# A two-block transformer step on one NeuronCore: joints by token tile, packed narrow weight blocks, and moved gate blocks, rotations and side work

## The reference, cut

```python
# layer 0: gated linear attention, 4 heads
proj = h @ w_in                         # q, k, v, gate and 16 low-rank columns
gk = gk_low @ w_gk2 + b_gk
log_a = jax.nn.log_sigmoid(gk) / 16.0   # cumulated in chunks of 64
o = rms_norm(o, g_onorm)
y = (o * jax.nn.silu(gate)) @ w_out
x = x + rms_norm(y, g_post)             # first joint
# layer 1: latent attention, 16 heads
c_q, c_kv, k_rope, gate = split(h @ w_in, [512, 1024, 1088])
q, kv = rms_norm(c_q) @ w_qb, rms_norm(c_kv) @ w_kvb   # rotations on q_rope, k_rope
p = softmax(mask(q @ k.T * scale)); o = p @ v
y = (o * jax.nn.silu(gate)) @ w_out
x = x + rms_norm(y, g_post)             # second joint
# layer 2: block-sparse attention and a gated delta rule (chunked,
# triangular inverse), merged by gates; then a gated feed-forward net
proj = rms_norm(x) @ w_in               # with 24 and 16 narrow gate columns
x = x + mixed @ w_o
x = x + (silu(h2 @ w_gate) * (h2 @ w_up)) @ w_down
return rms_norm(x, norm_f)
```

## Time and profile before

| | us |
|---|---|
| median of 3 runs (2389.57 to 2391.72) | 2390.56 |
| the profiled execution | 2388.96 |
| its span, first to last instruction | 2387.2 |
| TensorE busy in the span | 2332.0 |
| VectorE, ScalarE busy | 1467.7, 1298.3 |

### The profile page before, as it was taken

How to read it: one execution, slowest core, us unless ns; L and a number is a source line. 1 busy time by engine, 2 the same in 40 slices (tenths; PEclk the granted TensorE clock), 3 DMA queues, 4 the chain that set the end, 5 groups by cost and what they waited for, 6 DMA issues and landing times.

```text
span 2387.2 us, 33365 instructions
## 1 busy us (share of the span) xinstructions
PE 2332.0 (98%) x12514; PEld 1980.5 (83%) x12514; DVE 1467.7 (61%) x2567; ACT 1298.3 (54%) x2397; POOL 18.3 (1%) x38
## 2 busy tenths in 40 slices
PE   8999999899999899999999999999999999999998
PEld 7877788788888899778787888888888888888887
DVE  4554465665565655886777676656666666665554
ACT  5645455565565544775556555546555555554444
POOL 1000000000000000000000000000000000000000
PEclk9999999999999999999999999999999999999999
DMA  6555565556435465656554236656666666665564
GB/s 215 153 167 153 162 204 194 150 151 176 129 118 193 143 185 164 186 169 183 150 168 133 80 98 203 208 180 178 190 188 186 187 189 188 187 205 191 190 190 166
DMA packets 247403, 408.94 MB, mean 171 GB/s; under 512 B 29712, under 2 KB 62528, under 8 KB 246864
## 3 DMA queue, kind: packets, MB, share of 16 engines
q1 hardware_dynamic: 243392, 393.20, 54.4%
q0 software_dynamic: 3136, 10.26, 1.2%
q10 hardware_dynamic: 720, 3.42, 0.4%
HBM read 400.53 MB, written 6.29 MB: 170 GB/s over the span
## 4 chain that ended last, share of the span: by engine, by line
PE 90%; DVE 4%; ACT 4%; issue 1%; DMA 1%; SPq 0%; DVEq 0%; ACTq 0%; POOL 0%; POOLq 0%
PE banks L361 50%; PE banks L335 14%; PE banks L355 9%; PE banks L337 7%; DVE weights_low L306 1%; PE banks L804 1%; ACT weights_high L303 1%; PE banks L644 1%; PE banks L2221 1%; PE banks L2210 1%; PE banks L1681 1%; PE banks L815 0%; DMA weight_ring<-in_w_gla_in 0%; PE banks L1102 0%; PE banks L1112 0%
## 5 line engine op out<-in xcount | busy, mean ns | idle before, releaser
L306 DVE TENSOR_TENSOR weights_low<-weight_ring,weights_high 128x512 fp32r<-128x512 f32 (+3 forms) x1512 | 1006.6, 675 | 831.5 <-ACT weights_high L303 801.4
L303 ACT CAST weights_high<-weight_ring 128x512 fp32r<-128x512 f32 (+3 forms) x1512 | 910.3, 609 | 991.7 <-PE banks L361 624.9
L361 PE MATMUL banks<-weights_high,hidden_T 128*128 128x512 f32 x3008 | 863.9, 399 | 5.8 <-DVE weights_low L306 4.5
L361 PEld LDWEIGHTS banks<-weights_high,hidden_T 128*128 128x128 f32 x3008 | 556.2, 188 | 129.6 <-issue 10.8
L361 PE MATMUL banks<-weights_low,hidden_T 128*128 128x512 f32 x1504 | 466.2, 391 | 0.0
L335 PE MATMUL banks<-hidden_T,weights_high 128*128 128x512 f32 x1408 | 385.1, 394 | 0.6 <-DVE residual L2836 0.6
L361 PEld LDWEIGHTS banks<-weights_low,hidden_T 128*128 128x128 f32 x1504 | 283.0, 188 | 61.4
L335 PEld LDWEIGHTS banks<-hidden_T,weights_high 128*128 128x128 f32 x1408 | 240.4, 189 | 32.9 <-DVE residual L2836 0.8
L337 PEld LDWEIGHTS banks<-hidden_T,weights_low 128*128 128x128 f32 x1408 | 216.5, 189 | 30.3
L337 PE MATMUL banks<-hidden_T,weights_low 128*128 128x256 f32 x1408 | 224.4, 281 | 0.0
L355 PE MATMUL banks<-hidden_T,weights_high 128*128 128x256 f32 (+3 forms) x1120 | 185.8, 287 | 7.3 <-DVE weights_low L306 6.3
(11 more groups left out here) (401 smaller groups left out, 1731.1 us busy)
## 6 DMA issues: line engine op xcount, KB each, us to landing
weight_ring<-in_w_in SPq DMA_DIRECT2D x168, 512.0 KB, 3.6
weight_ring<-in_w_gla_in SPq DMA_DIRECT2D x96, 512.0 KB, 3.8
weight_ring<-in_w_gate SPq DMA_DIRECT2D x88, 512.0 KB, 3.6
weight_ring<-in_w_ffn_up SPq DMA_DIRECT2D x88, 512.0 KB, 3.6
weight_ring<-in_w_down SPq DMA_DIRECT2D x88, 512.0 KB, 3.8
weight_ring<-in_w_mla_in SPq DMA_DIRECT2D x49, 512.0 KB, 3.6
weight_ring<-in_w_gla_out SPq DMA_DIRECT2D x32, 512.0 KB, 3.9
weight_ring<-in_w_mla_out SPq DMA_DIRECT2D x32, 512.0 KB, 4.3
```

The lines of the kernel that those rows point to most:

```text
L303: nc.scalar.copy(hi, raw).then_inc(high_ready, 1)
L306: nc.vector.tensor_tensor(lo, raw, hi.bitcast(F32), ALU.subtract).then_inc(low_ready, 1)
L361: last = pe.matmul(ps[:, b + t, 0:width], a[:, t * P:(t + 1) * P], w, start=(k == 0 and n_th == 0), stop=(k == kt - 1 and n_th == 2))
```

## The change

- Narrow blocks are packed: on the host the columns are laid out so that four input tiles stand side by side (`PACK`), and a narrow chunk has 4 splits of four times the width in place of 16. TensorE issues the same 48 matmuls. The slots after them have lower numbers, so all positions are rewritten. The first block is loaded by ScalarE's queue, ahead of SyncE's.
- Start: the constants ahead are the identity alone, behind the gains, and a small activation stands first. All of x is turned in the first chunk's four packs.
- Joints: the last four tiles of the output product go one token tile after the other (`first_half`), and norm, add and turning go by token tile. The next product's first four splits stand between these steps.
- Gated attention: exponentials and logarithms two slots apart; two groups turned 4 and 2 tiles later.
- Latent attention: rotations one operation a slot; copies of turned heads 4 slots apart; TensorE's wait for the last value eviction in the second fill; the gate blocks of chunks 0 and 1 behind the exponentials of heads 4 and 8, that of chunk 2 at the end; fills 16 and 17 have two tiles, 24 and 30 none; the turning of heads moves from fills 17 to 27 to fills 19 to 29.
- Delta rule: one subtraction for both halves moves ahead of the wait, and fills are dealt out anew.

```diff
+        def packed_columns(w, width):
+            def piece(slot, k, n):
+                return slot.rearrange("p a n -> p (a n)")[:, 0:KD * width], w
+            return Gathered(1, piece), KD // PACK, 0, 0, PACK * width, hidden, PACKED
...
+            def load_first(self, eng):
+                w = self.chunks[0][0]
+                for n in range(w.pieces):
+                    eng.dma_start(*w.piece(ring[:, self.use0 % SLOTS, :, :], 0, n)).then_inc(landed[self.use0 % SLOTS], 16)
...
+                elif turned == PACKED:
+                    each = width // PACK
+                    for j in range(PACK):
+                        ahi, alo = acts(PACK * k + j)
+                        cs = slice(j * each, (j + 1) * each)
+                        for w, a, n_th in ((hi, ahi, 0), (hi, alo, 1), (lo, ahi, 2)):
+                            last = pe.matmul(ps[0:each, b, 0:S], w[:, cs], a, start=(k == 0 and j == 0 and n_th == 0),
+                                             stop=(k == kt - 1 and j == PACK - 1 and n_th == 2))
...
-                        by_halves = PARTS if first_half is not None and n + 1 == len(self.chunks) else 0
+                        by_halves = PARTS if first_half is not None and i == self.rounds - 1 and n + 1 == len(self.chunks) else 0
...
+            def turn_tokens(self, pe, g, tokens):
...
+                    if h in late:
...
+                        late[h]()
+                    else:
+                        fill()
...
-        const_head = sum(cols[name][1] for name in ("ident", "upto", "after", "ones"))
+        const_head = cols["ident"][1]
...
+        class PostNorm:
+            def place(self):
+                self.nth = planned["norm"] + 1
+                planned["norm"] += NT
+            def squared(self):
+                nc.scalar.sem_inc(squares, 1)
+            def inverse(self, t):
+                v, r = nc.vector, stat_x[:, t:t + 1]
+                v.wait_ge(squares, self.nth + t)
+                V(v.tensor_reduce(r, sums[:, t, :], AX, ALU.add))
+                V(v.tensor_scalar(r, r, 1.0 / D, EPS, ALU.mult, ALU.add))
+                V(v.reciprocal(r, r))
+                v.sem_inc(inverse, 1)
+            def root(self, t):
+                nc.scalar.wait_ge(inverse, self.nth + t)
+                Sc(nc.scalar.activation(stat_x[:, t:t + 1], stat_x[:, t:t + 1], ACT.Sqrt))
+                nc.scalar.sem_inc(rooted, 1)
+                nc.scalar.sem_inc(scaled[0], 1)
+            def ready(self, t):
+                nc.vector.wait_ge(rooted, self.nth + t)
+                nc.vector.sem_inc(scaled[1], 1)
+        post0, post1 = PostNorm(), PostNorm()
...
+            def begin_scalar(self, prod, after):
+                act, n = nc.scalar, len(prod.chunks) - 1
+                b = 2 * ((prod.chunk0 + n) % 2)
+                def squares_of(t):
+                    Sc(act.activation(junk[:, 0:W], ps[:, b + t, :], ACT.Square, accum_out=sums[:, t, D // W - 1:D // W]))
+                    act.sem_inc(chunk_squared, 1)
+                    self.post.squared()
+                act.wait_ge(first_done, self.n)
+                squares_of(0)
+                after.split(act, 0, 0, 0)
+                self.post.root(0)
+                after.split(act, 0, 0, 1)
+                prod.wait_done(act, prod.rounds - 1, n)
+                squares_of(1)
+                after.split(act, 0, 0, 2)
+                self.post.root(1)
+                after.split(act, 0, 0, 3)
...
+            def begin_vector(self, prod, after):
+                v = nc.vector
                 self.turns = self.turn.vector_steps()
-                self.add(0)
-                self.add(1)
+                self.post.inverse(0)
+                after.split(v, 0, 0, 0)
+                self.post.ready(0)
+                self.add(0, 0)
+                after.split(v, 0, 0, 1)
+                self.post.inverse(1)
+                after.split(v, 0, 0, 2)
+                self.post.ready(1)
+                self.add(0, 1)
+                self.add(1, 0)
                 next(self.turns)
-                self.add(2)
+                self.add(1, 1)
+                after.split(v, 0, 0, 3)
                 next(self.turns)
+                self.add(2, 0)
+                self.add(2, 1)
+                v.wait_ge(chunk_squared, NT * self.n * (D // W))
                 gained(prod, D // W - 1, 2 * ((prod.chunk0 + 1) % 2)).then_inc(chunk_evicted[(prod.chunk0 + 1) % 2], 1)
-                prod.wait_evicted(nc.vector)
-                self.add(3)
+                prod.wait_evicted(v)
+                for t in range(NT):
+                    self.add(3, t)
...
-                  164: lambda: gated((0, 1)), 180: lambda: gated((2, 3)), 200: lambda: gated((4, 5))}
+                  168: lambda: gated((0, 1)), 182: lambda: gated((2, 3)), 200: lambda: gated((4, 5))}
...
+        Q_SLOT = KD - PARTS
...
+        def mla_tiles(f):
+            return 2 if f < MLA_H + 2 else 0 if f in (24, 30) else 1
...
-            for n, norm in enumerate((norm_q, norm_kv)):
-                yield from pace.to(16 + 16 * n + 2)
-                prod_lat.wait_chunk(nc.scalar, n)
-                yield from pace.run(norm.scalar_steps(), 4)
-            yield from pace.to(50)
+            yield from pace.to(18)
+            prod_lat.wait_chunk(nc.scalar, 0)
+            yield from pace.run(norm_q.scalar_steps(), 4)
+            yield from pace.to(32)
+            prod_lat.wait_chunk(nc.scalar, 1)
+            yield from pace.run(norm_kv.scalar_steps(), 3)
             mla_tables_scalar()
...
+                if f == 1:
+                    prod_v.wait_evicted(pe)
...
+        def rope_side(ropes, first):
+            pace = Pace()
+            yield from pace.to(first)
+            yield from pace.run(ropes, 4)
...
+            def gate(n):
+                prod_mg1.wait_done(nc.scalar, 0, n)
+                c = prod_mg1.chunk0 + n
+                mla_gate_body(0, n, 2 * (c % 2)).then_inc(chunk_evicted[c % 2], 1)
+            attend.scalar(mla_fill(prod_mg1.split_fill(nc.scalar, None, 1, after=prod_mla_out), turns),
+                          {4: lambda: gate(0), 8: lambda: gate(1)})
+            gate(2)
...
+        def rotate_steps(x1, x2, c, s, t1, t2, out1, out2, single=False):
             v = nc.vector
             V(v.tensor_tensor(t1, x1, s, ALU.mult))
+            if single:
+                yield
             V(v.tensor_tensor(t2, x2, s, ALU.mult))
             yield
             V(v.tensor_tensor(out1, x1, c, ALU.mult))
+            if single:
+                yield
             V(v.tensor_tensor(out1, out1, t2, ALU.subtract))
...
-                    fill((2, 6)[hf])
+                    fill((3, 5)[hf])
+                for hf in HALVES:
+                    V(v.tensor_tensor(part_of(d_xt, hf), over(ident.unsqueeze(1), [P, NM // 2, P]), part_of(d_ct, hf), ALU.subtract))
                 if bt > 0:
                     inverses(bt - 1)
                 for hf in HALVES:
                     v.wait_ge(b_t1, t1_signalled(bt, 0, hf))
                     eye = over(ident.unsqueeze(1), [P, NM // 2, P])
                     V(v.tensor_tensor(part_of(d_x, hf), eye, bank(hf, 0), ALU.subtract))
-                    V(v.tensor_tensor(part_of(d_xt, hf), eye, part_of(d_ct, hf), ALU.subtract))
                     corner(1, hf)
                     v.sem_inc(b_xd, 1)
-                    fill((1, 2)[hf])
+                    fill((0, 3)[hf])
...
-            pool.wait_ge(low_ready, KD)
+            pool.wait_ge(low_ready, prod_gla.chunks[0][1] + 2)
...
+            act.dma_start(small["l0_pre"][:, :], A["small"]["l0_pre"]).then_inc(s_first, 16)
             act.dma_start(const[:, 0:const_head], A["const"][:, 0:const_head]).then_inc(s_first, 16)
-            act.dma_start(small["l0_pre"][:, :], A["small"]["l0_pre"]).then_inc(s_first, 16)
+            prod_gla.load_first(act)
             turns, gos = turn0.scalar_steps(), turn_go.scalar_steps()
             act.wait_ge(s_first, 32)
+            Sc(act.activation(stat[:, 60:61], ident[:, 0:1], ACT.Copy))
             for _ in range(2):
                 next(turns)
             prod_gla.prime(act)
-            prod_gla.run(act, range(13), gla_evict, prod_gla_out, gla_side_scalar(turns, gos))
+            for _ in turns:
...
-            prod_v.wait_evicted(pe)
```

183 lines of the change are left out of this document (91 added, 92 removed).

## The result

The changed kernel takes **2360.52 us** (median of 4 runs, 2357.74 to 2362.47) against 2391.14 before (2389.57 to 2391.81): a ratio of 0.9874, interval 0.9858 to 0.9889. That is 30.6 us faster, where 25.1 had been forecast. The profiled execution took 2357.74 us with a span of 2355.8; the one of before had a span of 2387.2, so the two traces differ by 31.4 us. Three executions in a far slower state of the chip (8313.5 us of joints_old, 2475.0 and 4713.6 us of exp_ln_alone) are left out of all medians here.

A forecast was written before the change was run, and what follows sets the result against it. TensorE, busy 98% of the span, was taken as the bound, so only its 55.2 us of idle and its half clock could be won. Ten terms summed to 25.1 us: 2363.9 profiled, 2365.5 on the runs' scale, range 2357 to 2377.

The forecast's parts named there:

- rival (b): Joints and after head 8: the clock does not fall; gain 4.8 us more, about 2361; chance 0.16.
- Start: Program start: first matmul at 4.7, copies 1.2 us later, first full-width matmul near 17; gain 4.5 us (2.5 to 5.5).
- Gated attention: Gated attention: turning first groups four tiles later wins 1.4 us; exponentials and logarithms two slots apart win 0.7 (0 to 1.6).
- The shift of two tiles: Gated attention: the other shift, of two tiles, has nothing to win.
- Joints: Two joints between layers: next product 2.25 us sooner each, less if half clock moves along; 4.5 for both (1.0 to 9.2).
- Narrow blocks: Packed narrow blocks: fewer splits win 3.8 us (2.5 to 3.8) in the key block, 1.0 in the delta rule's gate block.
- Rotations, copies, start of attention: Before latent attention: single-step rotations and moved copies win 2.1 us, the later value-eviction wait 1.9 (1.0 at least).
- Gate blocks: Latent attention: gate blocks behind exponentials of heads 4 and 8 win 3.1 us (0 to 5.1), despite a 1.5 stop at head 15.
- Delta rule: Delta rule: subtraction moved into idle time, weight split behind the second half; removes 1.06 us stops, gain 2.1 (-0.5 to 2.1).
- (a): Whole program: small stops behind `weights_low` come back elsewhere; half of all terms but the start, 2375 us; chance 0.18.
- (c): Joints, heads 8 to 15, start: shorter but more stops keep bringing half clock; slower, six new stretches give 2397; chance 0.03.
- (d): Joints and heads 8 and 9: interleaved splits and late tiles give back the start's gain; nothing measurable, 2388; chance 0.03.

The follow-up runs named there:

- joints_old: Changed kernel with both joints as in the kernel before (both token tiles at once, last four tiles not by token tile); 2363.85 us, ratio 0.9885.
- exp_ln_alone: Kernel before with one edit: exponentials and logarithms of the gated decays two slots apart instead of one; 2387.79 us, ratio 0.9985.
- start_order: Changed kernel with the transposes of x's third and fourth blocks each one pack of narrow matmuls earlier; 2355.65 us, ratio 0.9853.
- joint_warm: Changed kernel with eight matmuls of unread result (128 rows by 512 columns) added where TensorE stands at each joint; 2360.21 us, ratio 0.9872.
- rotations_paired: Changed kernel with latent attention's query rotations again two instructions a step; 2359.73 us, ratio 0.9875.
- tile_table_old: Changed kernel with the earlier table of tiles in latent attention, gate blocks still behind the exponentials; 2355.89 us, ratio 0.9856.
- changed_again: Changed kernel run once more without edits, as base beside later runs; 2359.64 us, ratio 0.9865.

## Why the prediction was right, point by point

The direction, the range (2357 to 2377) and the places held; the sum was 5.5 us short. How it was short matters: the forecast took idle time off the list, 23 us of it, and 21.5 went; but 9.9 us of what the profile calls busy time went as well, where the sum had under 3. Half of that were parts of stops that the profile draws as busy, and half was half clock, of which a part was luck. The time fell on rival (b)'s figure, about 2361, though what (b) said did not happen: the clock fell at both joints. The prediction's ends do not follow from its own bounds: the low ends come to 11.0 us, 2379.6 and not 2382, the high ones to 33.7, 2356.9.

- **Start**: forecast 4.5, in the two profiled executions 3.1. The table load ahead of any wait and the copies 1.2 us after the first matmul came as reckoned. Two terms were too small: the constant landed at 5.5, not 4.7, and ScalarE waited 2.75 us for transposes, not 1.5. The kernel before varies there too (21.80 and 23.32 in its own and exp_ln_alone's trace, 17.6 to 18.7 after), so 4.5 is inside what the runs give. The order of the transposes was not thought of: start_order won about another 1.5.
- **Gated attention**: 2.1 forecast, 4.6 measured. The small stops were given 0.7 of a shown 1.31; they were worth 2.4 (exp_ln_alone). Two steps failed: half of the shown idle time was written off without a reason, and all of it would still have been 1.1 short, since shown idle time is not the price of a stop. The shift of two tiles, said to have nothing to win, took away a stop of 0.23 at 292.64, which is the second of the two in the earlier trace rows.
- **Joints**: 2.25 each forecast, 2.6 standing time won. The half clock did not move along whole: at the first joint it gave 1.45 back against an old joint, at the second it depends on the execution. The forecast's bounds, 1.1 and 2.25 a joint, name this question rightly. The clock fell at both joints in all eleven traces without added matmuls, so rival (b) did not happen; joint_warm shows that it would have needed TensorE to be busy. That at full clock TensorE would wait for VectorE instead, so that at the first joint half clock cost 1.5 and not 3.0, was in no term.
- **Narrow blocks**: 3.8 forecast for the key block, 3.4 measured, and 4.0 if the first joint's clock is taken out of the same distance (6.0 us of product work at half clock behind 418.43, 4.7 behind 428.75 before: 0.6 us). No stop is left in this block or in the delta rule's.
- **Rotations, copies, start of attention**: 4.0 forecast, 6.6 measured. 4.3 us of it were shown as idle; seven stops hide 1.2 more, and shorter ones probably the rest. The reason given, two instructions a step, was wrong: rotations_paired shows that the pairs cost nothing once the key's rotation is split up. The copies and the moved wait were not undone alone.
- **Gate blocks**: 3.1 forecast, 3.6 measured. Of both, 1.7 forecast and 1.4 by distance are the half clock behind head 8, which the forecast tied to the stop of 2.4. exp_ln_alone has this stop without the half clock, so that term came true by luck of the execution; the stops alone gave 2.1. The place behind the exponentials works, and the stop at head 15 came with 1.27 for 1.5. The forecast put the stop to the moved copies and the missing cover; tile_table_old shows that the empty slot makes it, and that the doubled slots 16 and 17 were not needed.
- **Delta rule**: 2.1 forecast, 2.2 for the whole rest of the program. No run undid this part; both stops of 1.06 are gone from every trace with the change. A stop of 1.06 stands at 1442.60 in the first trace. At the same matmul it is 0.22 in the kernel before, 1.12 in exp_ln_alone and 0.48 in changed_again, so it is no property of the change.
- **Rivals (a), (c) and (d)**: the stops did not move on, and the clock fell nowhere in heads 8 to 15.

## What to carry to other kernels

Price a stop of a pipelined engine by the distance between the starts on both sides of it less the normal pace, not by the idle time shown: here that adds 0.17 us to each and finds stops that the list leaves out. When an edit changes several things in one stretch, undo each: of the attention part, one piece (the new table of tiles) cost 1.5 us and another (the rotations in single steps) did nothing. Before crediting an edit with a clock that stayed up, look whether it stays up in a trace without the edit. Before filling idle time to hold the clock, see which engine is second: at full clock VectorE took back half of the gain.

## What the runs showed of the hardware that was not expected

Half clock came in lengths of 3.4, 6.8 and 10.2 us, and for the same instructions the length differed between executions, which moves the whole kernel by about 1.5 us a step. It came at both joints in every trace without added matmuls. It also came with rows of small matmuls that have no stop at all, beginning between 2.0 us before their end and 1.2 behind it: four with 16 rows (3.6 us at full clock), in eleven of the thirteen traces that have them in a row; 32 with 16 columns (3.5 us), in nine of fourteen. With the decay matmuls spread over four tiles it did not come, in one trace. What decides between the traces in which it came and those in which it did not was not found.
